# Opening of a recurrence, retention and expert layer: three PSUM pairs for the turns, a low part by GpSimd, other orders

## What is computed

```python
h = concatenate([meta, x])
z = rmsnorm(h, norm_mix) @ w_in
y_a = rwkv7_mix(z[..., :P_A], ...)       # shift with mu, decays, recurrence
y_b = retention_mix(z[..., P_A:], gn_w_b)
h = h + concatenate([y_a, y_b]) @ w_out
u = rmsnorm(h, norm_ffn)
h = h + hier_moe(u, ...)                 # 32 experts, top 1 group, top 2 experts
return rmsnorm(h, norm_final)[:, N_META:]
```

## Time and profile before

| | |
|---|---|
| runs | 1349.95 us median of 3 (1349.08, 1349.95, 1355.18) |
| profiled execution | 1349.9 us, span from first to last instruction 1347.8 us |
| TensorE busy | 1283.3 us, 95% of the span |
| VectorE busy | 1028.1 us, 76% |
| ScalarE busy | 717.8 us, 53% |
| GpSimd busy | 560.7 us, 42% |
| stages | `project` to about 450 us, `mix` to about 735, experts to 1347.8 |

### The profile page before, as it was taken

One profiled execution on the slowest core, in us unless ns is written; L12 is line 12 of the kernel. 1 busy time (PEld: TensorE's weight loads), 2 busy tenths in 40 slices (PEclk: granted clock), 3 DMA queues, 4 the chain that ended last, 5 costly groups with the idle time before them and its releaser, 6 DMA issues. The chain is left out here.

```text
span 1347.8 us, 23900 instructions
## 1 busy us (share of the span) xinstructions
PE 1283.3 (95%) x9822; PEld 1106.0 (82%) x9822; DVE 1028.1 (76%) x1153; ACT 717.8 (53%) x820; POOL 560.7 (42%) x203
## 2 busy tenths in 40 slices
PE   5999999999999979999998799999999999999995
PEld 5899999999999768888875688888888788888882
DVE  5456566589988166777766799998998997777786
ACT  5435424212432253334324677787777777787754
POOL 1011011000000041111121777778779779999982
PEclk9999999999999889999999899999999999999998
DMA  6136665772434696656646999999999999999998
GB/s 237 37 137 162 183 192 158 235 231 85 153 98 113 236 292 192 194 174 210 200 145 227 420 416 410 403 412 408 410 407 414 407 410 410 409 414 415 411 344 294
DMA packets 155508, 374.06 MB, mean 278 GB/s; under 512 B 53376, under 2 KB 108672, under 8 KB 143248
## 3 DMA queue, kind: packets, MB, share of 16 engines
q1 hardware_dynamic: 143328, 329.35, 66.9%
q0 software_dynamic: 6912, 25.17, 5.4%
q10 hardware_dynamic: 5184, 18.35, 3.3%
HBM read 299.67 MB, written 73.17 MB: 277 GB/s over the span
## 5 line engine op out<-in xcount | busy, mean ns | idle before, releaser
L1236 PE MATMUL ps<-u_hi,w_hi 128*128 128x352 f32 (+1 forms) x720 | 237.5, 330 | 4.9 <-DVE u_lo L891 4.9
L1236 PE MATMUL ps<-u_lo,w_hi 128*128 128x352 f32 (+1 forms) x720 | 233.6, 324 | 0.0
L1236 PE MATMUL ps<-u_hi,w_lo 128*128 128x352 f32 (+1 forms) x720 | 232.6, 323 | 0.0
L1236 PEld LDWEIGHTS ps<-u_hi,w_hi 128*128 128x128 f32 x720 | 137.3, 191 | 10.5 <-issue 5.8
L1236 PEld LDWEIGHTS ps<-u_hi,w_lo 128*128 128x128 f32 x720 | 137.2, 191 | 0.0
L1236 PEld LDWEIGHTS ps<-u_lo,w_hi 128*128 128x128 f32 x720 | 137.1, 190 | 0.0
L1693 POOL TENSOR_TENSOR mix_stat<-mix_stat,minus_half 128x4 f32<-128x4 f32 x8 | 10.7, 1336 | 283.0 <-DVE mix_stat L2071 282.9
L3328 PE MATMUL ps<-first_up_hi,x_hi 128*128 128x512 f32 x256 | 103.0, 402 | 5.1 <-issue 2.9
L3328 PE MATMUL ps<-first_gate_hi,x_hi 128*128 128x512 f32 x248 | 98.8, 398 | 5.8 <-DVE x_lo L3100 5.4
L3328 PE MATMUL ps<-first_up_hi,x_lo 128*128 128x512 f32 x256 | 100.2, 392 | 0.0
L3328 PE MATMUL ps<-down_hi,hid_hi 128*128 128x512 f32 x248 | 99.3, 400 | 0.0
(11 more groups left out here) (478 smaller groups left out, 3432.3 us busy)
## 6 DMA issues: line engine op xcount, KB each, us to landing
first_down_raw<-in_moe_w_down SPq DMA_DIRECT2D x16, 2048.0 KB, 10.8
second_up_raw<-in_moe_w_up SPq DMA_DIRECT2D x16, 2048.0 KB, 9.8
down_raw<-in_moe_w_down SPq DMA_DIRECT2D x16, 2048.0 KB, 11.0
gate_raw<-in_moe_w_gate SPq DMA_DIRECT2D x15, 2048.0 KB, 10.2
up_raw<-in_moe_w_up SPq DMA_DIRECT2D x15, 2048.0 KB, 9.2
second_gate_raw<-in_moe_w_gate SPq DMA_DIRECT2D x15, 2048.0 KB, 10.7
y_slots<-y_out ACTq DMA_DIRECT2D x31, 512.0 KB, 11.4
w_raw<-in_w_in SPq DMA_DIRECT2D x30, 512.0 KB, 4.5
```

What stands on the lines that cost most here:

```text
L1236: mm = pe.matmul(z_of(n, r_), w[n % 3][:, k_, :], a[:, k_, c0:c1], start=(k_ == 0 and i == 0), stop=(k_ == KD - 1 and i == 2))
```

## The change

All of it is in the opening of `project`.

- Turns use three pairs of banks, 2-3, 4-5 and 6-7, in turn (`turn_bank`), so a turn waits for the low part of tile t - 3.
- The low part of block 0's weights is made by GpSimd, between the powers of tiles 3 and 4, with a semaphore of its own, `first_w_lo`.
- SP loads tile 3 ahead of block 0's weights and tile 4 ahead of block 1's.
- The first unit is a function of its own: 8 matmuls `w_hi, u_hi`, then 8 `w_lo, u_hi`, then 8 `w_hi, u_lo`, each group behind its own wait.
- Eight matmuls of the identity by itself stand ahead of `turn(0)` and four ahead of the first unit (`warm`). Their result is not used.
- `turn(6)` stands ahead of unit (1,0), no longer behind it.
- ScalarE and VectorE take tiles 4 to 8, the second and third weight blocks and the first scalings in another order. The words that come with the change also name tiles 2 and 3 as squared first; on ScalarE `square(2)` and `square(3)` stand where they stood, on both sides of `high(0)`.

```diff
+        def turn_bank(t):
+            return 2 + 2 * (t % 3)
...
                 load_x(2)
+                load_x(3)
                 load_w(0)
-                load_x(3)
+                load_x(4)
                 load_w(1)
                 sp.dma_start(fp[:], d["fm_params"]).then_inc(sem("fp_loaded"), 16)
-                for t in range(4, NT):
+                for t in range(5, NT):
                     load_x(t)
...
                     pool.tensor_tensor(stat[0:w, 2, t:t + 1], stat[0:w, 1, t:t + 1], half[0:w, 0:1], ALU.pow
                                        ).then_inc(sem("rstd_ready"), 1)
+                    if t == 3:
+                        pool.wait_ge(sem("w_hi_ready"), 1)
+                        pool.tensor_tensor(w_lo[0][:], w_raw[0][:], w_hi[0][:].bitcast(F32), ALU.subtract).then_inc(sem("first_w_lo"), 1)
...
                 def turn(t):
-                    w, b_ = N_META if t == 0 else P, 3 + 2 * (t % 2)
-                    if t >= 2:
-                        pe.wait_ge(sem("u_lo_ready"), t - 1)
+                    w, b_ = N_META if t == 0 else P, turn_bank(t)
+                    if t >= 3:
+                        pe.wait_ge(sem("u_lo_ready"), t - 2)
...
+                def warm(n):
+                    for _ in range(n):
+                        pe.matmul(ps[:, 0, 0:P], ident, ident, start=True, stop=True)
+
+                def first_unit():
+                    pairs = ((w_hi, u_hi), (w_lo, u_hi), (w_hi, u_lo))
+                    pe.wait_ge(sem("w_hi_ready"), 1)
+                    pe.wait_ge(sem("u_hi_ready"), 4)
+                    for i, (w, a) in enumerate(pairs):
+                        if i == 1:
+                            pe.wait_ge(sem("first_w_lo"), 1)
+                        if i == 2:
+                            pe.wait_ge(sem("u_lo_ready"), 4)
+                        for k_ in range(KD):
+                            mm = pe.matmul(z_of(0, 0), w[0][:, k_, :], a[:, k_, RANGES[0][0]:RANGES[0][1]],
+                                           start=(i == 0 and k_ == 0), stop=(i == 2 and k_ == KD - 1))
+                    mm.then_inc(sem("z_ready"), 1)
+
+                warm(8)
                 turn(0)
                 turn(1)
                 turn(2)
                 turn(3)
-                weights(0)
-                pe.wait_ge(sem("u_hi_ready"), 4)
-                pe.wait_ge(sem("u_lo_ready"), 4)
-                unit(0, 0)
+                warm(4)
+                first_unit()
                 turn(4)
                 turn(5)
+                turn(6)
                 weights(1)
                 unit(1, 0)
-                turn(6)
```

More of the change, by code:

```diff
@@ L576, in high @@
                     w = N_META if t == 0 else P
-                    b_ = 3 + 2 * (t % 2)
+                    b_ = turn_bank(t)
                     act.wait_ge(sem("u_turned"), t + 1)
@@ L716, in _ @@
                 high(2)
+                high(3)
                 square(4)
-                high(3)
                 split(1)
-                for t in range(4, 7):
-                    square(t + 1)
-                    high(t)
+                square(5)
+                square(6)
+                high(4)
+                high(5)
+                high(6)
+                act.wait_ge(sem("fp_loaded"), 16)
                 scaled(0, 0)
+                square(7)
                 scaled(1, 0)
+                square(8)
                 lora_tanh(0)
                 gate_tanh(0)
-                square(8)
+                split(2)
                 high(7)
-                split(2)
                 high(8)
@@ L916, in _ @@
                 low_rows(2)
-                low(0)
                 low_rows(3)
+                norm(4)
                 low(1)
+                norm(5)
+                norm(6)
+                low_rows(4)
+                low_rows(5)
+                low_rows(6)
                 dve.wait_ge(sem("fp_loaded"), 16)
@@ L923, in _ @@
                 dve.tensor_scalar(one_less_ka, raw["k_a"], -0.5, 1.0, ALU.mult, ALU.add).then_inc(sem("derived"), 1)
-                norm(4)
-                for t in range(4, 7):
-                    norm(t + 1)
-                    low_rows(t)
+                norm(7)
                 dve.wait_ge(sem("derived"), 3)
@@ L930, in _ @@
                 shift(0, 0, lora)
+                norm(8)
                 shift(1, 0, g_t)
                 gate_half(0)
-                norm(8)
+                low(2)
                 low_rows(7)
-                low(2)
                 low_rows(8)
@@ L1241, in weights @@
                     pe.wait_ge(sem("w_hi_ready"), n + 1)
-                    pe.wait_ge(sem("w_lo_ready"), n + 1)
+                    pe.wait_ge(sem("w_lo_ready"), n)
                 def lora_ups(q, r_):
```

## The result

The changed kernel took 1338.6 us (median of 4 runs, 1336.92 to 1340.3) beside 1351.58 for the kernel before (4 runs, 1349.08 to 1355.18): ratio 0.9923, 95% interval 0.9901 to 0.9946, so faster by more than 0.5%. The forecast was 1345.6, with a range from 1341.8 to 1351.5. The profiled execution took 1337.6 us, its span is 1335.3 (1347.8 before).

A forecast was written before the change was run, and what follows sets the result against it. TensorE was taken to bound the kernel, waiting only in the opening. Gains of 2.46 (wait), some 1.7 (clock) and 2.5 (earlier start), less 2.3 of new waits, made 4.3: 1349.9 - 4.3 = 1345.6 us, range 1341.8 to 1351.5.

The forecast's parts named there:

- turns 2 and 3: Opening on TensorE: both at the high clock after warming, turn(3) from 15.5 to 16.5 us, about 1 us long.
- the powers priced at 1.63 each: GpSimd in the opening: powers of tiles 5 and 6 beside VectorE's work, 1.63 us each instead of 0.55 alone.
- the waits before turns 5 and 6: New TensorE waits in the opening for normalised tiles 5 and 6: 1.6 and 0.7 us, 2.3 lost in the sum.
- B: Rival: warming doesn't warm, turns 2 and 3 stay at 1.97 us each; gain 3.3, 1346.6 us, chance 0.18.
- C: Rival: GpSimd's subtraction meets VectorE's normalisation and takes 5.5 us; gain 3.3, 1346.6 us, chance 0.10.
- the warming costs tile 3 one microsecond: Opening: the eight identity products delay turn(0), so tile 3 is normalised at 15.5 us against 14.5 before.
- 1.7 us of gain: Sum's term for the first unit no longer running partly at the low clock: some 1.7 of the 4.3 us.
- from there each row about 4.3 us earlier up to the last expert: Everything behind unit(0, 2), near 40.1 us: the opening's 4.3 us gain is kept to the end.
- D: Rival, slower: the clock falls at more places in the projection; four more falls give 1352.0 us, chance 0.12.
- E: Rival: the projection's two clock falls vanish, 3.2 us less; 1342.4 us, chance 0.12.
- The rigidity: Behind 50 us TensorE hardly waits, so a microsecond it gains before then should reach the end.
- the 2.46 in the sum: Sum's term for removing TensorE's wait before unit(0, 1): 2.46 of the 4.3 us.

The follow-up runs named there:

- r4_after_a: The changed kernel unedited, run again for a fourth trace of it; 1339.02 us.
- r2_after: The changed kernel unedited, run again beside the kernel before; 1340.42 us (12 runs), ratio 0.9952 to the kernel before.
- r3_dvelow: The changed kernel with the low part of block 0's weights back on VectorE instead of GpSimd; 1340.47 us (one run).
- r1_nowarm: The changed kernel without the eight and four identity products; 1341.86 us (6 runs), ratio 0.9958 to the kernel before.
- r2_turn6: The changed kernel with turn(6) put back behind unit(1, 0); 1340.35 us (one run).

## Why the prediction was wrong

**The opening came out.** Warming from 7.42 to 11.14 (forecast 7.5 to 10.9), tile 3 normalised at 15.72 (15.5), GpSimd's subtraction 2.36 us and done at 18.51 (2.4 and 18.0), all of the first unit at the high level in 3.92 us (3.9), unit (1, 0) at 26.79 (26.7), unit(0, 1) at 30.71 (30.5), the last low part ahead of unit(0, 2) at 40.18 (39.9) and that unit at 40.28 (40.1). Within it two terms were off and cancelled, which is luck: turns 2 and 3 end at 17.29, not 16.5, since the clock rose during turn(3) and not from turn(2) on (in `r4_after_a` turn(2) took 1.09 us, and there the unit started at 17.64 and ended at 21.57, as forecast), so the unit starts and ends 1.1 us later (0.2 of it because tile 3's square, sum and copy took 1.45 us up to its power, not 1.3); and the powers priced at 1.63 each took 1.82 for both, so the waits before turns 5 and 6 were 1.15 and some 0.2, not 1.6 and 0.7 (in `r2_after` they were 1.13 and 0.66). GpSimd's 2.36 us stand against 1.22 on VectorE in `r3_dvelow`, and cost nothing, since the unit wants `w_lo` only after its first eight matmuls. By the Trainium skill, GPSIMD Engine Reference, section 4.1, GpSimd is about twice as slow as VectorE at elementwise work with two inputs; these rows agree.

**Rivals B and C fell**: the unit was fast from its first matmul (B was right for turn(2) alone), and the subtraction met no reading of two SBUF tiles. That "the warming costs tile 3 one microsecond" was right, and its consequence was missed: without it (`r1_nowarm`) the new order is ready 1.5 us earlier. The forecast's sum gave the clock 1.7 us of gain, where the warming was worth -1.5 in this order and +1.4 in the old one.

**The step that failed** is the one from the opening to the end: "from there each row about 4.3 us earlier up to the last expert", with the clock falls of the rest kept aside as rivals D and E, from one trace that had two in the eight places of the projection. The rigidity holds in the changed kernel, where 4.3 us put in came out as 3.9; in the kernel before they came out as 4.1 against all its runs and as 2.1 against those of the same rounds. But the sum put the change in clock falls at nothing, and took their number from one execution. Over six traces of the old order and twelve of the new, the time lost to the clock between 50 and 530 us is 11.9 and 7.2 us on average. That is 4.7 us less, where the sum lacks 8.1 - 4.3 = 3.8; over all runs and the whole span, by the mean clocks, it is 4.0 less. So E's sign was right, and D's was wrong. But E's own mechanism, both falls of the projection gone, was seen in no trace: every one of the new order still has one or two from 50 to 300 us (1.7 or 3.4 us), against two to four in the old order, and half of what was saved lies behind 300 us, which neither rival looked at. A further piece lies in the opening: the trace that the forecast was made from was one of two in seven without a fall behind the 2.46 us wait. Removing that wait also removes 1.7 us in most executions, which adds about 0.9 us (5 of 7 against 2 of 11, times 1.7) to the 2.46 in the sum. With it the parts of the traces make 4.1 + 0.9 + 4.7 - 0.5 (behind 530 us) = 9.2 us, for 8.1 measured, and those of all runs 4.1 + 4.0 = 8.1, which is nearer than their uncertainty of 1 us deserves.

**What stays open** is why the falls behind 50 us are fewer in the new order. It is no matter of position alone: the changed kernel delayed by 4.3 us still lost 6.8 us there, and 18.7 in all over 12 runs. But the kernel before with the same delay also lost only 6.8, in one trace, and 20.6 in all over 12 runs, for 23.5 (25.1 in the same rounds); so position may play a part in the old kernel. Warming alone in the old order lost only 18.7, the new order without warming 20.9. Every version that was tried lost less than the kernel before, and no single part of the change carries it by these runs.

**The range** was built from the prices of mechanisms and had no term for the spread of the executions. One kernel's runs spread over 1340.7 to 1356.0 us, with a standard deviation of 3.05 us, and medians of whole groups of runs of before differ by 3.8 us. Three runs within 6 us had looked like a closeness that isn't there. The measured 13 us (four runs each) is itself 5 us more than the 8.1 of all runs; at 1340.5, the mean of all, the range from 1341.8 would still have missed it, by 1.3. These 1.3 us are the base: the forecast was subtracted from 1349.9, while the kernel before has a mean of 1348.65. Of the 7.0 us between 1345.6 and the measured 1338.6, 3.8 are the missing gain, 1.3 the base, and 1.9 the luck of four runs of the changed kernel below its mean.

**The best version** is the changed kernel without the two warmings (1340.1, 12 runs, unit(0, 1) at 29.2 us) or with them (1340.5, 24 runs): the opening prefers the former by some 1.5 us, the runs don't tell them apart.

## What to carry to other kernels

Take several traces of the kernel before, note in each where TensorE's granted clock rises and falls, and price an edit against their mean: a wait costs its own length and, as often as one is seen there, a clock fall. The mean granted clock of every run splits a difference into clock and the rest where traces are few. Compare a variant with the kernel before of the same rounds: the means of before moved by almost 3 us between groups. Products that warm the array paid here where TensorE would wait anyway; ahead of the first turn of the new order they stood in the way of tile 3 and cost more than the clock gave. A third buffer and a turn drawn forward took away 1.3 and 2.4 us here, the engine swap for one subtraction nothing.

## What the runs showed of the hardware

With a TensorE wait of 2.46 us before unit(0, 1) the granted clock was at half behind it (0.63 us for the first matmul instead of 0.40, save in `r2_turn6`, where it fell a microsecond later) in five of the seven traces that have it, each time costing 1.7 us; four traces of one and the same kernel differ in it, so the program alone doesn't fix it. In two of these four the clock had risen by turn(3) and fell again at 17 us; in the other two turn(3) still ran at the low level. The same kernel took 1340.73 to 1350.7 us in 12 runs of one group, and its time follows its mean clock (-0.66 over 95 runs). Eight products of the identity took 3.72 us at the start (0.46 each, two records) and four took 1.06 at 17.29, once the clock had risen. GpSimd's subtraction of 128x1024 took 2.36 us beside VectorE's reading of PSUM, and 5.51 beside its reading of SBUF twice.
